# A hybrid trunk with product-key experts: 128 tokens instead of 64 take their experts row by row, the dense expert matmuls get 448 columns instead of 512

## The reference

```python
q = (tb @ w_q).reshape(PEER_BLOCK, PEER_HEADS, 2, PEER_HALF)        # 8 heads, 2 halves of 128
s = jnp.einsum('thik,hink->thin', q, sub_keys)                      # 128 keys per half
s_top, i_top = lax.top_k(s, 16)
cand = s_top[:, :, 0, :, None] + s_top[:, :, 1, None, :]            # 256 sums per head
best_s, best_c = lax.top_k(cand, 16)
eid = i1 * N_KEYS + i2                                              # 128 x 128 = 16,384 experts
g = jax.nn.softmax(best_s, axis=-1)
act = jax.nn.gelu(einsum('thkd,td->thk', u_tab[eid], tb))           # 8 x 16 = 128 picks per token
out = einsum('thk,thkd->td', g * act, v_tab[eid])
```

## Time and profile before

| | |
|---|---|
| time, median of 3 runs | 2729.02 us (2724.49 to 2730.33) |
| the profiled execution, its own time | 2728.77 us |
| its span, first to last instruction | 2726.8 us |
| granted TensorE clock, mean | 0.979 |
| busy: PE / DVE / POOL / ACT | 2629.0 / 1711.4 / 1235.1 / 811.5 us |
| DMA over the span | 460.49 MB, mean 169 GB/s |
| expert phase begins (first scores) | about 1129 us |
| gate stage (first gates to last gates) | 1457.1 to 1915.7 us |
| output units | 1982.5 to 2702 us |

### The profile page before, as it was taken

One profiled execution on the slowest core, in us unless ns is written; L12 is line 12 of the kernel. 1 busy time (PEld: TensorE's weight loads), 2 busy tenths in 40 slices (PEclk: granted clock), 3 DMA queues, 4 the chain that ended last, 5 costly groups with the idle time before them and its releaser, 6 DMA issues.

```text
span 2726.8 us, 38609 instructions
## 1 busy us (share of the span) xinstructions
PE 2629.0 (96%) x14608; PEld 2275.3 (83%) x14608; DVE 1711.4 (63%) x2880; ACT 811.5 (30%) x968; POOL 1235.1 (45%) x659
## 2 busy tenths in 40 slices
PE   7899999999989989999998999999989999999997
PEld 6899999976779989988887888888878888888885
DVE  5785445444774330399887777775257777777663
ACT  2221213321021011233334544444323233333331
POOL 3455334322424544455553444443445555555442
PEclk8999999999989989999999999999999999999998
DMA  3223222234542222244445888986767776666541
GB/s 129 79 78 134 94 86 93 89 140 167 197 144 82 87 97 85 90 162 166 162 172 169 257 246 251 255 249 189 236 258 250 248 252 248 246 246 216 192 154 58
DMA packets 264023, 460.49 MB, mean 169 GB/s; under 512 B 144481, under 2 KB 144865, under 8 KB 257377
## 3 DMA queue, kind: packets, MB, share of 16 engines
q1 hardware_dynamic: 56496, 204.76, 21.7%
q10 hardware_dynamic: 188976, 187.01, 21.5%
q0 software_dynamic: 18432, 67.12, 6.8%
HBM read 365.17 MB, written 93.66 MB: 168 GB/s over the span
## 4 chain that ended last, share of the span: by engine, by line
PE 91%; DVE 5%; DMA 2%; issue 1%; ACT 1%; POOL 1%; ACTq 0%; DVEq 0%; POOLq 0%
PE ps L771 50%; PE ps L541 28%; PE ps L816 4%; PE ps L680 1%; PE ps L710 1%; PE ps L688 1%; PE ps L567 1%; DMA activation_scratch<-ge 1%; PE ps L784 1%; PE ps L692 1%; PE ps L695 1%; PE ps L668 0%; DVE v_lo L1444 0%; PE ps L673 0%; DVE cv_a L1460 0%
## 5 line engine op out<-in xcount | busy, mean ns | idle before, releaser
L517 POOL TENSOR_TENSOR w_lo<-raw,w_hi 128x1024 fp32r<-128x1024 f32 x128 | 319.6, 2497 | 378.5 <-PE ps L771 378.4
L517 POOL TENSOR_TENSOR w_lo<-raw,e_hi 128x1024 fp32r<-128x1024 f32 x128 | 311.9, 2437 | 394.8 <-PE ps L771 387.8
L491 POOL TENSOR_SCALAR w_hi<-raw 128x1024 fp32r<-128x1024 f32 x129 | 141.1, 1094 | 643.0 <-issue 512.5
L771 PE MATMUL ps<-p_hi,w_lo 128*128 128x512 f32 x1024 | 402.3, 393 | 0.0
L771 PE MATMUL ps<-g_hi,w_lo 128*128 128x512 f32 x1024 | 401.4, 392 | 0.0
L493 POOL TENSOR_TENSOR w_lo<-raw,w_hi 128x1024 fp32r<-128x1024 f32 x129 | 320.4, 2484 | 10.8
L541 PE MATMUL ps<-h_hi,w_hi 128*128 128x296 f32 (+1 forms) x1296 | 297.2, 311 | 18.3 <-ACT stage L913 9.4
L1677 DVE TENSOR_TENSOR abuf<-abuf,gbuf 128x512 f32<-128x512 f32 x128 | 268.2, 2095 | 70.5 <-DMA gbuf<-gate_scratch 50.7
L541 PE MATMUL ps<-h_lo,w_hi 128*128 128x296 f32 (+1 forms) x1296 | 283.2, 300 | 0.0
L541 PE MATMUL ps<-h_hi,w_lo 128*128 128x296 f32 (+1 forms) x1296 | 282.9, 300 | 0.0
L541 PEld LDWEIGHTS ps<-h_hi,w_hi 128*128 128x128 f32 x1296 | 212.7, 192 | 41.8 <-issue 24.5
(11 more groups left out here) (283 smaller groups left out, 5010.5 us busy)
## 6 DMA issues: line engine op xcount, KB each, us to landing
raw<-units SPq DMA_DIRECT2D x385, 512.0 KB, 3.3
activation_scratch<-ge ACTq DMA_DIRECT2D x128, 256.0 KB
gate_scratch<-gt ACTq DMA_DIRECT2D x32, 1024.0 KB, 6.9
abuf<-activation_scratch ACTq DMA_DIRECT2D x32, 1024.0 KB, 7.3
gbuf<-gate_scratch ACTq DMA_DIRECT2D x32, 1024.0 KB
prev<-ssm_in ACTq DMA_DIRECT2D x8, 1024.0 KB, 5.6
ssm_s<-prev ACTq DMA_DIRECT2D x8, 1024.0 KB, 4.4
parked_tiles<-stage ACTq DMA_DIRECT2D x24, 296.0 KB, 2.1
```

Source lines behind the costliest of these rows:

```text
L491: pool.tensor_scalar(w_hi[:, s, :], raw[:, r, :], 1.0, 1.0, ALU.mult, ALU.mult).then_inc(s_whi, 1)
L517: pool.tensor_tensor(w_lo[:, n % 2, :], raw[:, n % RAW, :], e_hi[m % HS_].bitcast(F32), ALU.subtract)\
L771: last = mm(accp[par], w[:, k * P:(k + 1) * P], x_[:, k, t0:t0 + ND], start=k == 0 and i == 0, stop=k == KT - 1 and i == 2)
```

## The change

128 tokens are handled by rows (the 64 sampled and the last 64 of the prompt), 448 densely. What follows from it in the code:

- The row-wise tile now has all 8 heads on 128 partitions, so it takes 128 gathers per table and not 64. Of the dense tokens the last tile has 64, with 4 heads on each half. UT gives 14, 16, 16, 16 and 8 units to the five tiles.
- 28 gate blocks, seven of them followed by one unit and 21 by two; 9 activation units are left after them (M_GATE = 119).
- The one-hots are three wide DVE instructions per block and no small ones.
- `gt` holds 32 tokens in two buffers; there is one store of 2 MB for every two blocks, in pieces of 512 B.
- The ring has 6 gather buffers. Dot products stand inside the top-k tiles (13, 13, 13 and 5 of them) and 3 stand behind each gate block. The row sums stand ahead of the gate multiply, one for every output unit. The order of the gathers comes from `read_by()`.
- The second buffer of the pick extraction is gone; its two halves run one after the other.
- The gate stage's loop on PE and ACT is written out.
- The picks are turned by plain float32 matmuls; the row sums are copied and turned just ahead of the last group, in 8 transposes.

```diff
-NS = TS
+NS = P
-TT = [(ND, PH // 2)] + [(t, PH) for t in range(0, ND, P)]
+TT = [(ND, PH)] + [(t, PH) for t in range(0, ND - HALF, P)] + [(ND - HALF, PH // 2)]
+SB = 2 * TB
-UT = [6, 12, 12, 12, 12]
+UT = [14, 16, 16, 16, 8]
-M_GATE = M_TOP + 2 * NB
+UB = [2 if b % 4 else 1 for b in range(NB)]
+M_BLOCK = [M_TOP + sum(UB[:b]) for b in range(NB + 1)]
+M_GATE = M_BLOCK[-1]
-UG = 4
-N_PICK = PH // 2 * TOPK
-N_DOT0 = 12
-V_AT = (0, 2, 4, 6, 7)
+UG = 6
+N_PICK = PH * TOPK
+DOTS_T = [0, 13, 13, 13, 5]
+DOTS_B = 3
...
+def read_by():
+    at = []
+    for j, n in enumerate(DOTS_T):
+        at += [M_TILE[j] + (i + 1) * UT[j] // n for i in range(n)]
+    for b in range(NB):
+        at += [M_BLOCK[b] + UB[b]] * len(dots_of(b))
+    return at + [NKEYS - GI + k for k in range(N_PICK)]
 def gathers_after(m):
+    if m == UT[0] + 1:
+        return range(UG)
+    return [j + UG for j, c in enumerate(READ_BY) if max(c + 2, UT[0] + 2) == m and j + UG < 2 * N_PICK]
...
-                    for i in range(3):
-                        last = pe.transpose(S0[:, i * P:(i + 1) * P], pick[:, i, :], ident[:])
+                    parts = [slice(0, P)] if TT[j][1] == PH else [slice(0, HALF), slice(HALF, P)]
+                    for i in range(3):
+                        for p_ in parts:
+                            n = p_.stop - p_.start
+                            last = mm(S0[p_, i * P:i * P + n], pick[p_, i, 0:n], ident[p_, p_], start=True, stop=True)
...
+            outputs(NG - 2, 0)
             pe.wait_ge(s_osb, 1)
             for k in range(KT):
-                last = mm(turned_rows[:, k * NS:(k + 1) * NS], osb[:, k * P:(k + 1) * P], pairs[:],
-                          start=True, stop=True)
+                last = pe.transpose(turned_rows[:, k], osb[:, k * P:(k + 1) * P], ident[:])
             last.then_inc(s_ot, 1)
-            for par in range(2):
-                outputs(NG - 2 + par, par)
+            outputs(NG - 1, 1)
...
+            def gates_out(b):
+                B, part_ = b // 2, b % 2
                 act.wait_ge(s_gm, b + 1)
+                if B >= 2 and part_ == 0:
+                    act.wait_ge(s_gs, 16 * (B - 1))
+                act.activation(gt[:, B % 2, :, part_ * TB:(part_ + 1) * TB].rearrange("p i t -> p t i"),
                                ps[:, 4:8, :].rearrange("p a (t i) -> p (a t) i", i=P),
                                ACT.Copy).then_inc(s_gt, 1)
+                if part_:
+                    act.wait_ge(s_gt, b + 1)
+                    act.dma_start(gate_dram[:, :, B].rearrange("g p a -> p g a"),
+                                  gt[:, B % 2].rearrange("p (g i) t -> p g (i t)", g=2 * NG)).then_inc(s_gs, 16)
...
                 if m == M_GATE:
-                    act.wait_ge(s_gs, 16 * NB)
+                    act.wait_ge(s_ud, N_PICK)
+                    act.activation(dots[:], dots[:], ACT.Gelu).then_inc(s_act, 1)
+                    act.wait_ge(s_gs, 16 * (NB // 2))
                     for hb in range(2):
                         load_half(0, hb)
...
+            group(NG - 2, 0, True)
+            group(NG - 1, 1, False)
             act.wait_ge(s_ud, 2 * N_PICK)
             act.activation(osb[:].rearrange("p (a t) -> p a t", a=2), acc_rows, ACT.Copy).then_inc(s_osb, 1)
-            group(NG - 2, 0, True)
-            group(NG - 1, 1, False)
...
-                for j in range(TB):
-                    t = slice(t0 + j, t0 + j + 1)
-                    last = ts_(oh_g[:, par, j, :], iota[:], pickT[:, 0, t], pickT[:, 2, t], ALU.is_equal, ALU.mult)
-                last.then_inc(s_oh, 1)
+                across = iota[:].unsqueeze(1).to_broadcast([P, TB, P])
+                key_a, key_b, weight = (pickT[:, i, t0:t0 + TB].unsqueeze(2).to_broadcast([P, TB, P]) for i in range(3))
+                tt_(oh_g[:, par], across, key_a, ALU.is_equal).then_inc(s_dc, 1)
+                chain[0] += 1
+                tt_(oh_2[:, par], across, key_b, ALU.is_equal)
+                dve.wait_ge(s_dc, chain[0])
+                tt_(oh_g[:, par], oh_g[:, par], weight, ALU.mult).then_inc(s_oh, 1)
...
-                    v = a.rearrange("p (n t) -> p n t", t=TB)
+                    row_sum(g * GI + u)
+                    v = a.rearrange("p (n t) -> p n t", t=SB)
                     tt_(v, v, gbuf[:, u // 4, :, u % 4, :], ALU.mult).then_inc(s_pm, 1)
-                    k = sums_at(g, u)
-                    if k is not None:
-                        row_sum(k)
```

More of the change, by code:

```diff
@@ L820, in _ @@
             pe.wait_ge(s_pks, len(TT) - 1)
[L821 to L825, removed]
-                for par in range(2):
[L827 to L830, removed]
+            for b in range(NB):
+                gates(b, b % 2, b == 0)
+                for m in range(M_BLOCK[b], M_BLOCK[b + 1]):
+                    activations(m)
             for m in range(M_GATE, NKEYS):
@@ L1139, in _ @@
                     act.wait_ge(s_pkT, j)
-                    act.activation(pickT[:, :, TT[j][0]:TT[j][0] + P],
-                                   S0[:, 0:3 * P].rearrange("p (a t) -> p a t", a=3), ACT.Copy).then_inc(s_pks, 1)
-            def gates_out(b, stored):
+                    n = P if heads == PH else HALF
+                    act.activation(pickT[:, :, TT[j][0]:TT[j][0] + n],
+                                   S0[:, 0:3 * P].rearrange("p (a t) -> p a t", a=3)[:, :, 0:n],
+                                   ACT.Copy).then_inc(s_pks, 1)
@@ L1166, in _ @@
-            for b in range(NB - 4, NB):
-                gates_out(b, 16 * b)
-                if b == NB - 4:
-                    act.wait_ge(s_ud, N_PICK)
-                    act.activation(dots[:], dots[:], ACT.Gelu).then_inc(s_act, 1)
-                for c in range(2):
-                    activated(M_TOP + 2 * b + c)
+                if part_:
+                    act.wait_ge(s_gt, b + 1)
+                    act.dma_start(gate_dram[:, :, B].rearrange("g p a -> p g a"),
+                                  gt[:, B % 2].rearrange("p (g i) t -> p g (i t)", g=2 * NG)).then_inc(s_gs, 16)
@@ L1174, in load_half @@
+            for b in range(NB):
+                gates_out(b)
+                for m in range(M_BLOCK[b], M_BLOCK[b + 1]):
+                    activated(m)
             def load_half(g, hb):
@@ L1541, in _, with top16 @@
             dve.wait_ge(s_h, 2 * KT)
[L1542 to L1543 removed]
+            tt_(g_sum[:], *sample_cols, ALU.add).then_inc(s_gp, 1)
             dve.wait_ge(s_out, 48)
[L1545 to L1547 removed]
+            def top16(vals, idx, src, rows, between):
                 for i in range(rows):
@@ L1551, in top16 @@
                 link(last)
+                between()
                 for i in range(rows):
+                    if 2 * i == rows:
+                        between()
                     dve.max_index(idx[:, i, 0:8], vals[:, i, 0:8], src[:, i, :])
@@ L1582, in _, with between @@
                 rows, np_ = 2 * heads, heads * TOPK
+                due = [*range(sum(DOTS_T[:j]), sum(DOTS_T[:j + 1]))]
+                def between():
+                    if due:
+                        row_dot(due.pop(0))
                 dve.wait_ge(s_scs, j + 1)
-                top16(top, topi, sc, rows)
+                top16(top, topi, sc, rows, between)
                 dve.sem_inc(s_scf, 1)
@@ L1630, in _ @@
                     dve.wait_ge(s_eid, 1)
-                elif j < 4:
-                    for d in range(UG * (j - 1), UG * j):
-                        row_dot(d)
+                while due:
+                    between()
             def one_hots(b, par):
```

103 lines of the change are left out of this document (29 added, 74 removed).

## The result

The median went from 2726.76 us (four runs, 2723.78 to 2730.33) to **2611.82 us** (four runs, 2605.44 to 2620.0): a ratio of 0.958, 95% interval 0.9548 to 0.9611. That is 115 us less. I had predicted 2569, and 2611.82 lies above the range that I gave (2554 to 2604). The profiled execution took 2613.84 us, with a span of 2612.0.

What follows compares the result with a forecast made beforehand. The prediction took PE, busy for 96% of the span, to bound the kernel. Its terms, led by -164.5 us for expert matmuls, summed to -159.9 from 2728.8, so 2569 us, range 2554 to 2604.

Steps and rivals of the forecast that it cites:

- expert matmuls: All expert units: 6144 matmuls lose 64 columns each, at 0.421 ns a column; -164.5 us.
- gate stage over PE's pace: Gate blocks: DMA engine time of 187 to 206 us against 192 makes the stage just about full; +5 us.
- seam and what follows it: Last gates to output units: PE stands for w_lo behind gathers that wait for row sums; about +13 us, 0 to 25.
- gates, loop, picks, one-hots, top-k tiles, output units, last group: Smaller terms: gates -14.3, loop -3.4, picks +2.0, one-hots +0.5, top-k tiles and output units nothing, last group +1.5 us.
- the straight line to 0.302: Expert matmuls: lower bound on a column's price, in ns, from the line down to the 128-column gate matmul; 119 us saved.
- the gathers have some 11 us of slack: Gate stage: room of the gathers against the one-hots, counted against the stage becoming bound by DMA.
- rival 2: Gate stage becomes bound by DMA; with gates at 83 us per MB, 40 us more, about 2600 us; chance 0.16.
- The 7.2 us stop of before: First output units: PE's old stop goes, as half of group 1 loads behind the last activation store; -7.2 us.
- Rivals 3: Output units: DVE's chain grows past a unit, 0.3 us over 4.88, 128 times, about 2607 us; chance 0.08.
- 5: Output units: p_lo too falls behind a w_lo in each, 8.7 us a unit, about 3050 us; chance 0.02.
- Rival 4: Expert matmuls: columns worth less, 2614 us by the line to 128 columns, 2682 by the skill's page; chance 0.05.

Runs made afterwards that it cites:

- experiments 4: Only half of the gates stored, the other half being a copy of it, against the kernel after: 2610.08 us, ratio 0.9581.
- 7: 256 B instead of 4 KB fetched per row in 78 gathers of the gate stage, on top of experiment 1: 2592.72 us, ratio 0.9517.
- experiment 10: Kernel after with first row sums ahead of loads, early gathers, group 0 loads split, gate stores on SP's queue and small one-hots: 2569.28 us, ratio 0.9409.
- experiment 1: First six row sums moved ahead of the loads of group 0, against the kernel after: 2591.06 us, ratio 0.9503.
- experiment 3: 78 gathers of the gate stage left out, dot products kept, against the kernel after: 2592.79 us, ratio 0.9505.
- experiments 9: As experiment 10 but with the wide one-hots of the kernel after: 2575.18 us, ratio 0.9434.
- experiment 12: Output units' matmuls cut to 384 columns from 448, against the kernel after: 2612.17 us (two runs), ratio 0.9571.

## Why the prediction was wrong

The sign, the stages and most terms held; three terms were off, all to one side.

| term | predicted us | measured us |
|---|---|---|
| expert matmuls | -164.5 | -155 |
| gate stage over PE's pace | +5 | +26 |
| seam and what follows it | +13 | +25 to +26 |
| gates, loop, picks, one-hots, top-k tiles, output units, last group | as given | as given, within some 3 us together |

2568.9 + 9.5 + 21 + 12.5 = 2612, against 2613.8 in the profile; 2 us have no place.

1. **The price of a column, right in kind, off in size.** I took 227.7 ns for 512 columns from the piece of 48 beside gate blocks. That piece is too short by what overlaps with its neighbour: in the top-k stage before, the chain's pieces add up to 1224 matmuls in 282.45 us, 230.8 ns each, and after, to 1680 in 345.20, 205.5 each. So a matmul gave 25.3 ns for 64 columns, 0.395 ns a column, and 6144 of them 155 us (151 if the output units' half goes by their own step, 230.2 to 206.2). I had the straight line to 0.302 as the other bound, and the value is near the end that I took. The 8.3 ns that I had worked out for these columns from the Trainium skill's two figures ("TensorE: Matmul & The Clock Gate", "Back-to-back issue gap") is three times too small here.

2. **The gate stage, the step that failed.** "I take +5 us; 0 if gates cost 47, 45 if they cost 83" treated it as a balance of DMA engine time. That balance was sound: q10's 35.7% of 16 engines over 356 us are 2034 us, less 10.8 MB of activation stores at 45, so 57 us for a MB of gates where I had 64, and the share was 0.88. But experiments 4 and 7 take bytes away and gain some 3 us each, and experiment 10 keeps the bytes and loses the 26 us. They come from the **order in which things are issued**, and from what the engines do to each other there; three chains share them: gathers issued late, for which DVE waits in order with the next one-hots behind; the gathers and w_lo stretched beside wide one-hots; and ACT standing 4.3 to 12.3 us at the issue behind a 2 MB store, which I had at nothing though it stood 2.1 to 2.4 us behind the 1 MB stores before. Removing all three gives the stage back (332.2 us, PE's pace being 329.6), removing the first or the second alone gives nothing beyond the scatter (the SP stores were tried neither alone nor with late gathers). I had costed the wide one-hots by DVE's 6.9 us a block, which holds (2.2 us each), but only when POOL is away: with it 3.73 and 4.41 us (at 1680.72 and 1686.65 above). I wrote "the gathers have some 11 us of slack", and never asked what POOL and DVE do to each other in that slack. The row for it was there: the multiply at 2.17 us beside w_lo and 0.69 alone. How the 26 us divide among the three was not settled; the gains depend on their order. The sign that I had set for rival 2, gate blocks over 12.3 us with DVE waiting for gathers or ACT for stores, came true at 13.05 us, but not its cause: late issue gives the same sign as full DMA engines.
   The Trainium skill, "SBUF — State Buffer", section "Who interferes with whom", says that a DVE instruction with two SBUF inputs contends with GpSimd instructions that read SBUF, and calls the ports that the two share an exclusive lock. The trace agrees for w_lo (2.4 to 4.22 us) and the one-hots. That section's inference that such instructions leave the making of DMA descriptors alone does not fit the gathers' 0.94 to 2.84 us at issue.

3. **The seam: the right queue, too short.** Named in the prediction and shown by experiment 1: POOL's gathers wait for row sums (28.7 + 12.2 us) and PE for w_lo (19.3 us, longest 8.3, where I had worked out 8.2) and then for p_lo (8.6, where I had 5), 29 us of idle in all where I had "some 20". What I left out is stores that land late in ACT's queue. A Gelu waits 7.4 us for its buffer, whose store stands behind the last 2 MB of gates, and only then does ACT issue the loads of group 0: the first row sum starts 34 us after the last gates (1893.2) and not 27, and PE's first long stop is 7.7 us and not 3. A later Gelu waits 8.8 us for a store behind these four loads (13.8 in experiment 1). And the clock, 0.85 over 91 us, costs 7 us and not 4. The 7.2 us stop of before went, as forecast.

4. **What held.** Output units: in the kernel after, DVE's chain takes 4.3 us of 4.95 (I wrote 4.4 of 4.88), as this timeline shows from x to p_lo's end and to the next x:

```profile
2203.23 0.62 DVE L1657 TENSOR_TENSOR x<-x,ps 128x448 f32<-128x448 f32 x1 [0.69 <-PE ps L773]
2204.07 1.29 DVE L1569 SCALAR_TENSOR_TENSOR ps<-ug,coef,ps 128x1024 f32<-128x1024 f32 x1 [0.21 <-DVE x L1657]
2205.26 0.96 DVE L1670 TENSOR_TENSOR abuf<-abuf,gbuf 128x448 f32<-128x448 f32 x1
2206.87 0.62 DVE L1672 TENSOR_TENSOR p_lo<-abuf,p_hi 128x448 fp32r<-128x448 f32 x1 [0.65 <-ACT p_hi L1171]
2208.19 0.62 DVE L1657 TENSOR_TENSOR x<-x,ps 128x448 f32<-128x448 f32 x1 [0.70 <-PE ps L773]
```

   Rivals 3 and 5 fall by it. The last group's 1.06 and 0.92 us on ACT stand at 2543.65 as predicted, and first one-hots and top-k tiles cost what I said. Rival 4's sum by the line to 128 columns, 2614, comes within 3 us of the median for a wrong reason: its price was 119 us and the rows say 155.
   The range failed with the term. I gave +45 at most to the gate stage, but then let 2604 stand as its end, and did not add seam and column price on the same side.

## What to carry to other kernels

In this kernel a saved matmul column was worth its 0.40 ns only where the engines beside PE kept up with it. When units shrink, count not only each engine's busy time and the bytes, but whom each queue's head waits for, and which instructions slow each other when they meet. If removing one suspect gives nothing, remove them in pairs before calling it innocent: here the second removal gave 8 to 12 us of the stage, where single ones gave nothing that could be told. And a stage's length in one profile has a scatter: look at it first in versions that leave the stage alone. Row sums, gathers or stores that need nothing of a load should not be ordered behind it.

## What the runs showed of the hardware that I had not expected

- Wide two-input instructions of DVE (128x2048 elements, 2.2 us) and POOL's work stretch each other: the one-hot to 4.4 us and more, w_lo from 2.4 to 4.2, and the issue of a gather from 0.94 to 3.0.
- The issue of a DMA by ACT is not free behind a big one: 0.34 us otherwise, 4.3 to 12.3 us for a 224 KB store right behind a 2 MB store in the kernel after, and 2.1 to 2.4 behind a 1 MB store in the kernel before. With the gathers left out (experiment 3) it was 4.2 to 5.25 us, so moving the gathers is part of the long ones. With the gate stores on SP's queue (experiments 9 and 10) it was 0.34 each time.
- Gate packets of 512 B cost about 57 us of engine time a MB (worked out above), those of 256 B 79 as the prediction worked out, long ones 44 to 46.
- Stops cost twice: in experiment 12 the first 17 matmuls after a stop of 4.58 us took 5.57 us (2200.33 to 2205.90), where 177.1 ns each make 3.0.
